# The first expert's operand from selection products on TensorE instead of a gather through HBM

## The chip, the cores and the metric

One core of one Trainium2 chip runs the whole program. The metric is the device time of one execution in microseconds (us). The kernel before took 1873.63 us in the median of 3 runs (1872.92 to 1876.07). Its profiled execution took 1871.54 us, with a span of 1869.7 us from the first to the last recorded instruction.

## The reference

Two blocks of a network work on 256 tokens of width 1024. What matters here is the last layer, a mixture of experts: a router picks 2 of 8 experts for each token, and each expert is a gated feed-forward network of inner width 3584.

```python
def moe_swiglu(h, w_router, w_gate, w_up, w_down):
    logits = (h @ w_router).astype(jnp.float32)
    top_vals, top_idx = lax.top_k(logits, TOP_K)
    top_w = jax.nn.softmax(top_vals, axis=-1)
    combine = jnp.einsum('bsk,bske->bse', top_w,
                         jax.nn.one_hot(top_idx, N_EXPERTS, dtype=jnp.float32)).astype(h.dtype)
    out = jnp.zeros_like(h)
    for e in range(N_EXPERTS):
        out = out + combine[..., e:e + 1] * swiglu(h, w_gate[e], w_up[e], w_down[e])
    return out
```

`h` is the root-mean-square norm of the layer's input with the gain `od_norm_ffn`, and `swiglu(h) = (silu(h @ w_gate) * (h @ w_up)) @ w_down`. All is float32.

## The kernel before

**Order of the work.** Each engine has its own list of instructions, written out in the program, and the engines wait for each other on semaphores. There is no scheduler: what stands first in a list goes first. The dense layers come first; the expert stage begins at about half of the span and lasts to nearly its end.

**Weights.** All weights stream through SBUF in granules of 128 x 2048 float32 (1 MB). SyncE loads them into six slots (`wraw`, L547 in the expert stage). ScalarE makes a rounded copy `whi` (L1320), VectorE the remainder `wlo` (L1382, the helper `lo`); both have three slots. TensorE forms each product in three matmuls, high by high, low by high and high by low (`three`, L656 to L658). A `wraw` slot is loaded again after `lo_done`; a `whi` slot is written again after TensorE has used it.

**Experts.** Each expert works on up to 128 tokens. One expert is 42 granules (`BODY`), in the order of the table `MOE`: gate and up projections of one of seven column groups, and the down projection of the group before. Gate and up take the tokens as the stationary operand `xgh`, `xgl` (model width on the partitions, tokens along the columns). An overflow path, which is not taken in the profiled execution, repeats the loop for experts with more than 128 tokens.

**Routing.** After the last job of the attention output, TensorE makes the logits (L895) and turns the residual to token-major form (L902). VectorE ranks the logits (`selm`, L1868, marks the chosen pairs). TensorE counts with a triangular matrix of ones how many tokens stand ahead of each token (L914 to L918, `slot_mm`). VectorE turns the counts into row numbers `row` of a table in HBM (`first_row` is 128 (e + 1), so expert 0 owns the rows 128 to 255) and into the indices `idx` (L1885). It then scales the tokens by norm and gain into `htm` (L1892 and L1893, two tiles of 128 tokens, `h_rows`).

**Dispatch.** GpSimd writes the tokens of `htm` to their rows of `expert_rows` in HBM with four indirect DMAs (L636, semaphore `dispatched`, 16 for each). ScalarE waits for all four and loads the 128 rows of expert 0 into `xgt` (L1288, L1289). TensorE waits for that load and transposes it in eight pieces (`turn_inputs(0)`, L926), four into bank 7 and four into bank 1. ScalarE makes `xgh` (L1294, `inputs_hi`), VectorE `xgl` (`inputs_lo`). Then the loop over the experts begins. The rows of expert E + 1 are loaded by SyncE during expert E, at its twentieth turn (L543 to L545), and transposed near its end (L981).

Of the kernel before, what the change touches and what calls it, by code (L numbers as in the profile page):

```python
# [15 lines left out]
P = 128  # L16
T = 256
D = 1024
# [9 lines left out]
NE = 8  # L28
# [263 lines left out]
def program(nc, wall, x_d, params_d, consts_d, pos_d, onehot_d, relb_d, poolw_d, recip_d, bv_d, fgain_d,  # L292
# [6 lines left out]
    with ctx:  # L299
# [11 lines left out]
        def sem(name):  # L311
            return ctx.enter_context(nc.semaphore(name))
# [27 lines left out]
        KB = 1024  # L340
# [70 lines left out]
        atl = place("atl", [P, 2, 4, P], f32r, 12 * KB)  # L411
        htm = place("htm", [P, 2, D], f32, 16 * KB)
        xtm = place("xtm", [P, 2, D], f32, 24 * KB)
        mgain = place("mgain", [P, D], f32, 32 * KB)
        fgain = place("fgain", [P, D], f32, 36 * KB)
        sg = place("sg", [P, 2, 512], f32, 40 * KB)
        act_ = place("act_", [P, 512], f32, 44 * KB)
# [11 lines left out]
        wrow = place("wrow", [P, 4], f32, 46 * KB + 704)  # L429
        cnt = place("cnt", [P, NE], f32, 46 * KB + 768)  # L430
        tabled = place("tabled", [P, 1], f32, 46 * KB + 832)
        cmp1 = place("cmp1", [P, 2, NE, NE], f32, 47 * KB)
        cmp2 = place("cmp2", [P, 2, NE, NE], f32, 47 * KB + 512)
        xgt = place("xgt", [P, D], f32, 48 * KB)
# [8 lines left out]
        ident = con[:, CC["ident"]:CC["ident"] + P]  # L443
        before = con[:, CC["before"]:CC["before"] + P]
        first_row = con[:, CC["first_row"]:CC["first_row"] + 2 * NE]

        def pcol(name, i):
            return par[:, COL[name] + i:COL[name] + i + 1]
# [37 lines left out]
        tok_var, tok_std, h_rows = sem("tok_var"), sem("tok_std"), sem("h_rows")  # L486
        logit_mm, routed_max, routed_exp = sem("logit_mm"), sem("routed_max"), sem("routed_exp")
        rank_done, slot_mm, flag_ready, idx_ready = sem("rank_done"), sem("slot_mm"), sem("flag_ready"), sem("idx_ready")
        zeros_set, rows_zeroed, dispatched = sem("zeros_set"), sem("rows_zeroed"), sem("dispatched")
        xg_loaded, xgt_mm, xg_hi, xg_lo = sem("xg_loaded"), sem("xgt_mm"), sem("xg_hi"), sem("xg_lo")  # L490
        gu_done, parts_used = sem("gu_done"), sem("parts_used")
# [32 lines left out]
        @block.sync  # L524
        def _(sp):
            sp.dma_start(wraw[:, 0, :], wall[0, :, :]).then_inc(w_loaded[0], 16)
            sp.dma_start(xres[:], x_d).then_inc(x_loaded, 16)
            sp.dma_start(par[:], params_d).then_inc(par_loaded, 16)
            sp.dma_start(wraw[:, 1, :], wall[1, :, :]).then_inc(w_loaded[1], 16)
            sp.dma_start(con[:], consts_d).then_inc(con_loaded, 16)  # L530
            sp.dma_start(posi[:], pos_d).then_inc(con_loaded, 16)
            for g in range(2, GD + 2):
                if g >= NW:
                    sp.wait_ge(lo_done, g - NW + 1)
                sp.dma_start(wraw[:, g % NW, :], wall[g, :, :]).then_inc(w_loaded[g % NW], 16)

            def load_expert(E, back):
                for j in range(2, BODY + 2):
                    g = GD + j
                    if j == 12:  # L540
                        sp.wait_ge(y_out, E * 2 + 2)
                        sp.dma_start(rows_out[bass.ds(E * P, P), :], ysb[:]).then_inc(y_stored, 16)
                    if j == 20:  # L543
                        sp.wait_ge(xgt_mm, E * 2 + 2)
                        sp.dma_start(xgt[:], rows_in[bass.ds(E * P + 2 * P, P), :]).then_inc(xg_loaded, 16)  # L545
                    sp.wait_ge(lo_done, E * BODY + (g - NW + 1))
                    sp.dma_start(wraw[:, g % NW, :],  # L547
                                 wall[bass.ds(E * BODY + (g - back * BODY), 1), :, :].rearrange("g p n -> (g p) n")
                                 ).then_inc(w_loaded[g % NW], 16)

            with sp.Fori(0, NE) as E:
                load_expert(E, 0)
            sp.wait_ge(flag_ready, 1)
            over = sp.value_load(flag[0:1, 0:1])
            with sp.If(over > 0):
                with sp.Fori(NE, 2 * NE) as E:
                    load_expert(E, NE)
                sp.wait_ge(y_out, 4 * NE + 2)
                sp.dma_start(rows_out[2 * NE * P:(2 * NE + 1) * P, :], ysb[:]).then_inc(y_last, 16)
            with sp.Else():  # L560
                sp.wait_ge(y_out, 2 * NE + 2)
                sp.dma_start(rows_out[NE * P:(NE + 1) * P, :], ysb[:]).then_inc(y_last, 16)
            for t in range(2):
                sp.wait_ge(fin_out, t + 1)
                sp.dma_start(out_d[t * P:(t + 1) * P, :], outb[:, t, :]).then_inc(stored, 16)
            sp.wait_ge(stored, 32)
# [84 lines left out]
        def _(pe):  # L651
# [258 lines left out]
            by_token(KD - 1)  # L910
            pe.wait_ge(rank_done, 1)

            count = bank[7][:, 32:32 + 3 * NE]
            nc.tensor.matmul(count[:, 0:8], before, selm[:, 0, :], start=True, stop=True)  # L914
            nc.tensor.matmul(count[:, 8:16], before, selm[:, 1, :], start=True, stop=False)
            nc.tensor.matmul(count[:, 8:16], ones[:], selm[:, 0, :], start=False, stop=True)
# [9 lines left out]
                        mm = nc.tensor.transpose(bank[b][:, c * P:(c + 1) * P], xgt[:, k * P:(k + 1) * P], ident)  # L926
                    mm.then_inc(xgt_mm, 1)

            turn_inputs(0)
            pe.wait_ge(xtm_out, 4)  # L930

            def expert(E):
                def part(j, out, c, half, last):

                    s = (GD + j) % NS
                    pe.wait_ge(lo_done, E * BODY + (GD + j + 1))
                    for i in range(4):
                        k = 4 * half + i
                        w = slice(i * 512, (i + 1) * 512)
                        mm = three(out, xgh[:, k, :], xgl[:, k, :], whi[:, s, w], wlo[:, s, w], k == 0, k == 7)  # L940
                    mm.then_inc(gu_done if last else parts_used, 1)

                def turn(c):

                    pe.wait_ge(prod_done, E * FC + (c + 1))
                    for i in range(4):
                        mm = nc.tensor.transpose(bank[6][:, i * P:(i + 1) * P], act_[:, i * P:(i + 1) * P], ident)  # L947
                    mm.then_inc(t_done, 1)

                def down(j, c, half):  # L950
                    s = (GD + j) % NS
                    pe.wait_ge(at_lo, E * FC + (c + 1))
                    if c == 0 and half == 0:
                        pe.wait_ge(y_out, E * 2 + 2)
                    pe.wait_ge(lo_done, E * BODY + (GD + j + 1))
                    for i in range(2):
                        k = 2 * half + i
                        for n in range(2):
                            w = slice(i * D + n * 512, i * D + (n + 1) * 512)
                            mm = three(bank[4 + n], ath[:, c % 2, k, :], atl[:, c % 2, k, :], whi[:, s, w], wlo[:, s, w],  # L960
                                       c == 0 and k == 0, c == FC - 1 and k == 3)
                    mm.then_inc(parts_used, 1)


                pe.wait_ge(xg_hi, E * 2 + 2)
                pe.wait_ge(xg_lo, E * 2 + 2)
                for j, (kind, c, half) in enumerate(MOE):
                    if kind == "G":
                        if half == 0 and c >= 2:
                            pe.wait_ge(silu_done, E * FC + (c - 1))  # L970
                        part(j, bank[c % 2], c, half, half == 1)
                    elif kind == "U":
                        if half == 0 and c >= 1:
                            turn(c - 1)
                        if half == 0 and c >= 2:
                            pe.wait_ge(prod_done, E * FC + (c - 1))
                        part(j, bank[2 + c % 2], c, half, half == 1)
                    else:
                        if c == FC - 1 and half == 0:
                            pe.wait_ge(at_lo, E * FC + FC)  # L980
                            turn_inputs(E + 1)  # L981
                        down(j, c, half)
                        if c == FC - 2 and half == 0:
                            turn(c + 1)
# [16 lines left out]
        def _(act):  # L1001
# [283 lines left out]
            for t in range(2):  # L1285
                sc.activation(ex[:, t, :], lg[:, t, :], ACT.Exp, bias=rs[:, t:t + 1], scale=rtm[:, t:t + 1]
                              ).then_inc(routed_exp, 1)
            act.wait_ge(dispatched, 64)  # L1288
            act.dma_start(xgt[:], rows_in[P:2 * P, :]).then_inc(xg_loaded, 16)  # L1289

            def inputs_hi(E):
                for half, b in ((0, 7), (1, 1)):
                    act.wait_ge(xgt_mm, E * 2 + (half + 1))
# [74 lines left out]
        def _(v):  # L1368
# [6 lines left out]
            def link(ins):  # L1375

                ins.then_inc(vstep, 1)
                chain[0] += 1
                v.wait_ge(vstep, chain[0])
# [494 lines left out]


            v.wait_ge(slot_mm, 1)
            counts = bank[7][:, 32:32 + 2 * NE].rearrange("p (t e) -> p t e", t=2)
            ve.tensor_scalar(spill[:], counts, P - 0.5, float(P * (NE - 1)), ALU.is_gt, MUL)
            link(ve.tensor_tensor(row[:], counts, first_row.rearrange("p (t e) -> p t e", t=2), ADD))
            link(ve.tensor_tensor(row[:], row[:], spill[:], ADD))  # L1880
# [3 lines left out]
            link(ve.tensor_tensor(rr[:, :, 0], rsum[:], rr[:, :, 1], SUB))  # L1884
            ve.tensor_copy(idx[:], rr[:].rearrange("p t r -> p (t r)")).then_inc(idx_ready, 1)  # L1885

            v.wait_ge(tok_std, 1)
            link(ve.reciprocal(rtm[:], rs[:, 12:14]))
            v.wait_ge(gains_loaded, 32)
# [3 lines left out]
                ve.scalar_tensor_tensor(htm[:, t, 512:1024], bank[b], rtm[:, t:t + 1], mgain[:, 512:1024], MUL, MUL  # L1893
                                        ).then_inc(h_rows, 1)

            link(ve.tensor_copy(cnt[:], bank[7][:, 32 + 2 * NE:32 + 3 * NE]))
            link(ve.tensor_reduce(rs[:, 2:4], lg[:], AX.X, MAX))
            link(ve.tensor_tensor(rs[:, 2:4], rs[:, 2:4], rtm[:], MUL))
            ve.tensor_scalar(rs[:, 0:2], rs[:, 2:4], -1.0, None, MUL).then_inc(routed_max, 1)
# [187 lines left out]
```

## Time and profile before

| what | us |
|---|---|
| median of 3 runs | 1873.63 |
| lowest, highest | 1872.92, 1876.07 |
| profiled execution | 1871.54 |
| its span | 1869.7 |
| TensorE busy in the span | 1725.9 (92%) |
| VectorE busy | 1464.0 (78%) |
| ScalarE busy | 1167.8 (62%) |
| GpSimd busy | 122.8 (7%) |

The table shows how full the engines are over the whole span. A change at one place is judged by the chain that ended last around that place: the profile's chain of waits names for each step the work that released it. The granted clock of TensorE (PEclk) is 1.00 at 2.4 GHz and 0.50 at 1.2 GHz. Starts are in microseconds from the start of the span.

### The profile page before, as it was taken

How to read it: one execution, taken by the hardware profiler on the slowest of the kernel's cores; microseconds unless marked ns; L12 is line 12 of the kernel's file. 1: busy time of each engine (PE TensorE's matmuls, PEld its weight loads, DVE VectorE, ACT ScalarE, POOL GpSimd, SP SyncE). 2: the span in 40 equal slices, each digit the busy share in tenths (PEclk: the TensorE clock that was granted, in tenths of full speed). 3: DMA queues.
4: the chain of work that ended last, by engine and by line, in shares of the span. 5: the costliest groups of instructions: out<-in, count | busy, mean ns of one | idle time of the engine just before them, and what ended most of it. 6: DMA issues, size and time to landing. Idle time of an engine off the chain costs nothing.

```text
span 1869.7 us, 26590 instructions
## 1 busy us (share of the span) xinstructions
PE 1725.9 (92%) x10284; PEld 1529.7 (82%) x10284; DVE 1464.0 (78%) x1444; ACT 1167.8 (62%) x1154; POOL 122.8 (7%) x112
## 2 busy tenths in 40 slices
PE   7787899997799999874999999999999999999994
PEld 6777799997799999764888888888888888888883
DVE  7888788866766655653888888889888888888886
ACT  5424567754254444443778778787787877877774
POOL 1000054421020001001000000000000000000000
PEclk9988999998999999897999999999999999999997
DMA  7332378584445457223899999999999999999994
GB/s 295 146 112 91 128 290 356 186 194 192 155 158 181 181 201 247 93 69 124 322 382 349 406 378 368 383 358 408 375 366 380 365 393 373 357 409 363 386 370 173
DMA packets 75741, 517.08 MB, mean 277 GB/s; under 512 B 8016, under 2 KB 8400, under 8 KB 17168
## 3 DMA queue, kind: packets, MB, share of 16 engines
q1 hardware_dynamic: 68976, 489.75, 68.8%
q0 software_dynamic: 6544, 25.74, 4.6%
q8 instruction: 53, 0.87, 0.2%
q10 hardware_dynamic: 144, 0.52, 0.1%
q14 instruction: 24, 0.20, 0.0%
HBM read 491.87 MB, written 24.12 MB: 276 GB/s over the span
## 4 chain that ended last, share of the span: by engine, by line
PE 80%; DVE 11%; ACT 5%; issue 2%; DMA 1%; POOL 1%; DVEq 0%; POOLq 0%; SPq 0%; ACTq 0%
PE psum L656 25%; PE psum L658 25%; PE psum L657 25%; DVE wlo L1382 4%; ACT whi L1012 3%; DVE acc L1497 2%; PE psum L947 1%; DVE al L1423 1%; PE psum L926 0%; ACT s L1229 0%; PE psum L706 0%; DMA expert_rows<-htm,idx 0%; DMA par<-params 0%; PE psum L863 0%; DMA yrow<-expert_outs,idx 0%
## 5 line engine op out<-in xcount | busy, mean ns | idle before, releaser
L1382 DVE TENSOR_TENSOR wlo<-wraw,whi 128x2048 fp32r<-128x2048 f32 x456 | 1043.2, 2291 | 242.4 <-ACT whi L1012 122.7
L1320 ACT ACTIVATE whi<-wraw 128x2048 fp32r<-128x2048 f32 x336 | 643.5, 1918 | 213.5 <-PE psum L658 213.5
L656 PE MATMUL psum<-ah,whi 128*128 128x256 f32 x1176 | 342.6, 291 | 20.8 <-DVE al L1423 11.9
L656 PE MATMUL psum<-whi,xgh 128*128 128x512 f32 x896 | 357.6, 399 | 1.6 <-DVE xgl L1382 1.6
L658 PE MATMUL psum<-whi,xgl 128*128 128x512 f32 x896 | 351.9, 393 | 0.0
L657 PE MATMUL psum<-wlo,xgh 128*128 128x512 f32 x896 | 349.8, 390 | 0.0
L657 PE MATMUL psum<-al,whi 128*128 128x256 f32 x1176 | 336.0, 286 | 0.0
L658 PE MATMUL psum<-ah,wlo 128*128 128x256 f32 x1176 | 335.7, 285 | 0.0
L1012 ACT ACTIVATE whi<-wraw 128x2048 fp32r<-128x2048 f32 x118 | 225.2, 1910 | 149.3 <-PE psum L658 145.6
L656 PEld LDWEIGHTS psum<-ah,whi 128*128 128x128 f32 x1176 | 229.5, 195 | 24.8 <-issue 10.4
L657 PEld LDWEIGHTS psum<-al,whi 128*128 128x128 f32 x1176 | 229.4, 195 | 0.6
L658 PEld LDWEIGHTS psum<-ah,wlo 128*128 128x128 f32 x1176 | 229.0, 195 | 0.0
L658 PEld LDWEIGHTS psum<-whi,xgl 128*128 128x128 f32 x896 | 168.6, 188 | 38.5
L656 PEld LDWEIGHTS psum<-whi,xgh 128*128 128x128 f32 x896 | 168.9, 188 | 36.9 <-issue 2.0
L657 PEld LDWEIGHTS psum<-wlo,xgh 128*128 128x128 f32 x896 | 168.9, 188 | 35.3
L656 PE MATMUL psum<-whi,ath 128*128 128x512 f32 x448 | 177.4, 396 | 0.0
L658 PE MATMUL psum<-whi,atl 128*128 128x512 f32 x448 | 175.6, 392 | 0.0
L657 PE MATMUL psum<-wlo,ath 128*128 128x512 f32 x448 | 174.5, 389 | 0.0
L658 PEld LDWEIGHTS psum<-whi,atl 128*128 128x128 f32 x448 | 84.1, 188 | 19.2
L657 PEld LDWEIGHTS psum<-wlo,ath 128*128 128x128 f32 x448 | 84.2, 188 | 18.1
L656 PEld LDWEIGHTS psum<-whi,ath 128*128 128x128 f32 x448 | 84.2, 188 | 16.9
L656 PE MATMUL psum<-fh,whi 128*128 128x256 f32 x352 | 97.5, 277 | 0.0
(330 smaller groups left out, 2070.0 us busy)
## 6 DMA issues: line engine op xcount, KB each, us to landing
wraw<-weights SPq DMA_DIRECT2D x456, 1024.0 KB, 6.8
expert_rows<-zeros POOLq DMA_DIRECT2D x1, 8704.0 KB, 43.5
expert_outs<-ysb SPq DMA_DIRECT2D x9, 512.0 KB, 6.6
expert_outs<-zeros POOLq DMA_DIRECT2D x1, 4096.0 KB, 59.8
xgt<-expert_rows SPq DMA_DIRECT2D x8, 512.0 KB, 8.2
bias_rows<-ttab POOLq DMA_DIRECT2D x1, 3072.0 KB, 36.5
btab<-bias_rows POOLq DMA_DIRECT2D x1, 2048.0 KB, 12.1
xres<-x SPq DMA_DIRECT2D x1, 1024.0 KB, 6.9
```

Source lines behind the costliest of these rows:

```text
L656: nc.tensor.matmul(out, lh, rh, start=start, stop=False)
L657: nc.tensor.matmul(out, lh, rl, start=False, stop=False)
L658: return nc.tensor.matmul(out, ll, rh, start=False, stop=stop)
L947: mm = nc.tensor.transpose(bank[6][:, i * P:(i + 1) * P], act_[:, i * P:(i + 1) * P], ident)
L1012: sc.activation(whi[:, g % NS, :], wraw[:, g % NW, :], ACT.Copy).then_inc(hi_done, 1)
L1320: sc.activation(whi[:, g % NS, :], wraw[:, g % NW, :], ACT.Copy).then_inc(hi_done, 1)
L1382: return ve.tensor_tensor(dst, value, hi.bitcast(f32), SUB)
L1423: ve.scalar_tensor_tensor(al[:, c, :], xres[:, c, :], gain(c), ah[:, c, :].bitcast(f32), MUL, SUB).then_inc(h_lo, 1)
L1497: ve.scalar_tensor_tensor(acc[:, c, :], u[:, c, tap:tap + T], pcol("conv_dw_w", 4 * tap + c), acc[:, c, :], MUL, ADD).then_inc(conv_step, 1)
```

## The change

The operand of expert 0 is no longer read back from HBM. VectorE compares the row numbers of expert 0 with the numbers 128 to 255 and gets two 0/1 matrices `sel0` (tokens on the partitions, places along the columns). TensorE multiplies `htm` with them: for each of the eight 128-wide pieces of the model width, two float32 matmuls of 128 x 128 (one for each tile of tokens) add up in PSUM, which gives the pieces in transposed form in the same banks as before. The numbers 128 to 255 come with the gain, whose tile `mgain` grows by 128 columns and moves. The counts move from bank 7 to bank 3. The four indirect writes stay, and SyncE now waits for them ahead of the load of the rows of expert 1.

```diff
@@ sync, load_expert
                     if j == 20:
+                        sp.wait_ge(dispatched, 64)
                         sp.wait_ge(xgt_mm, E * 2 + 2)
                         sp.dma_start(xgt[:], rows_in[bass.ds(E * P + 2 * P, P), :]).then_inc(xg_loaded, 16)
@@ tensor
-            count = bank[7][:, 32:32 + 3 * NE]
+            count = bank[3][:, 32:32 + 3 * NE]
...
-            turn_inputs(0)
+            pe.wait_ge(sel_ready, 1)
+            pe.wait_ge(h_rows, 2)
+            for half, b in ((0, 7), (1, 1)):
+                for c in range(4):
+                    k = 4 * half + c
+                    for t in range(2):
+                        mm = nc.tensor.matmul(bank[b][:, c * P:(c + 1) * P], htm[:, t, k * P:(k + 1) * P], sel0[:, t, :],
+                                              start=(t == 0), stop=(t == 1))
+                mm.then_inc(xgt_mm, 1)
             pe.wait_ge(xtm_out, 4)
...
-                            turn_inputs(E + 1)
+                            turn_inputs(E)
@@ scalar
-            act.wait_ge(dispatched, 64)
-            act.dma_start(xgt[:], rows_in[P:2 * P, :]).then_inc(xg_loaded, 16)
-
@@ vector
             ve.tensor_copy(idx[:], rr[:].rearrange("p t r -> p (t r)")).then_inc(idx_ready, 1)
 
+            v.wait_ge(gains_loaded, 32)
+            ve.tensor_scalar(sel0[:, 0, :], rows0, row[:, 0, 0:1], None, ALU.is_equal)
+            ve.tensor_scalar(sel0[:, 1, :], rows0, row[:, 1, 0:1], None, ALU.is_equal).then_inc(sel_ready, 1)
             v.wait_ge(tok_std, 1)
```

On TensorE, between the counts (`selm`) and the first matmul of expert 0 (`whi`, `xgh`), the list before reads:

```order
L918 MATMUL psum<-selm,ones 128x8
L926 MATMUL psum<-con,xgt 128x128 [waits xg_loaded]
L926 MATMUL psum<-con,xgt 128x128 x7
L986 UNCONDITIONAL_BRANCH [waits xtm_out]
L986 ISA
L936 ISA [waits xg_lo,xg_hi]
L656 MATMUL psum<-whi,xgh 128x512 [waits lo_done]
```

And now (`sel_150` is `sel0`):

```order
L923 MATMUL psum<-selm,ones 128x8
L940 MATMUL psum<-sel_150,htm 128x128 [waits h_rows,sel_ready]
L940 MATMUL psum<-sel_150,htm 128x128 x15
L999 UNCONDITIONAL_BRANCH [waits xtm_out]
L999 ISA
L949 ISA [waits xg_lo,xg_hi]
L661 MATMUL psum<-whi,xgh 128x512 [waits lo_done]
```

Eight transposes that waited for a load give way to sixteen matmuls that wait for VectorE. On VectorE, from the indices to the tokens, the list before reads:

```order
L1884 TENSOR_TENSOR rr<-rsum,rr 128x2 [waits vstep]
L1885 CAST idx<-rr 128x4 [waits vstep]
L1888 RECIPROCAL rtm<-rs 128x2 [waits tok_std]
L1892 SCALAR_TENSOR_TENSOR htm<-xtm,rtm,mgain 128x512 [waits xtm_out,gains_loaded,vstep]
L1893 SCALAR_TENSOR_TENSOR htm<-psum,rtm,mgain 128x512
```

And now:

```order
L1894 TENSOR_TENSOR rr<-rsum,rr 128x2 [waits vstep]
L1895 CAST idx<-rr 128x4 [waits vstep]
L1898 TENSOR_SCALAR sel_150<-mgain,row 128x128 [waits gains_loaded]
L1899 TENSOR_SCALAR sel_150<-mgain,row 128x128
L1901 RECIPROCAL rtm<-rs 128x2 [waits tok_std]
L1905 SCALAR_TENSOR_TENSOR htm<-xtm,rtm,mgain 128x512 [waits xtm_out,gains_loaded,vstep]
L1906 SCALAR_TENSOR_TENSOR htm<-psum,rtm,mgain 128x512
```

The two comparisons stand ahead of everything that makes `htm`; the rest of VectorE's list is as before.

## Rows read from the trace of the kernel before

**Rows 1.** Stretches: length, busy PE, PEld, DVE, ACT, POOL, clock, DMA share, GB/s.

```profile
799.80:802.00 2.20, 1.55 (x8) 1.12 (x8) 2.13 (x3) 0.00 (x0) 0.00 (x0) 1.00 0.00 0
...
859.20:860.80 1.60, 0.00 (x0) 0.00 (x0) 1.45 (x6) 1.58 (x5) 0.00 (x0) 0.91 1.00 425
...
864.00:884.00 20.00, 0.00 (x0) 0.00 (x0) 8.03 (x26) 3.15 (x5) 5.77 (x4) 0.50 0.53 184
...
887.60:891.20 3.60, 3.60 (x9) 2.83 (x10) 1.22 (x1) 3.31 (x5) 0.00 (x0) 0.50 0.00 0
...
900.00:1840.00 940.00, 940.00 (x4252) 771.40 (x4251) 826.61 (x457) 718.93 (x492) 0.00 (x0) 1.00 0.97 375
```

**Rows 2.** Chain of waits, 865 to 892: start, us, what.

```profile
865.39 0.67 DVE htm L1893
...
872.66 7.81 DMA expert_rows<-htm,idx
880.50 3.49 DMA xgt<-expert_rows
884.03 1.98 PE psum L926 x8
886.03 0.60 ACT xgh L1294
886.66 0.70 DVE xgl L1382
887.37 0.23 issue
887.60 0.79 PE psum L656
```

**Rows 3.** Timeline, VectorE: start, us, engine, line, what.

```profile
860.61 0.17 DVE L1868 TENSOR_SCALAR selm<-rank 128x16 f32<-128x16 f32 x1
...
866.63 0.75 DVE L1893 SCALAR_TENSOR_TENSOR htm<-psum,rtm,mgain 128x512 f32<-128x512 f32 x1
...
872.48 0.17 DVE L1914 TENSOR_REDUCE wrow<-ex 128x2 f32<-128x16 f32 x1
...
889.98 2.29 DVE L1382 TENSOR_TENSOR wlo<-wraw,whi 128x2048 fp32r<-128x2048 f32 x1 [2.62 <-ACT whi L1320]
```

**Rows 4.** VectorE's groups by form.

```profile
L1816 DVE TENSOR_SCALAR s<-s,st 128x128 f32<-128x128 f32 x16 | 4.5, 284 | 0.3
```

**Rows 5.** The load of the gains: duration ns, start us.

```profile
L628 POOL DMA_DIRECT2D mgain<-expert_gain x1: 561/561/561, 835.4 to 835.4; - x1
```

**Rows 6.** Timeline, TensorE.

```profile
784.39 0.90 PE L863 MATMUL psum<-con,s 128*128 128x128 f32 x3 [1.09 <-DVE s L1816]
...
786.36 0.63 PE L875 MATMUL psum<-p2T,v 128*128 128x128 f32 x2
786.79 0.63 PE L874 MATMUL psum<-p2T,v 128*128 128x128 f32 x2
...
788.72 0.34 PE L658 MATMUL psum<-ah,wlo 128*128 128x256 f32 x1
...
799.85 0.46 PE L855 MATMUL psum<-k,q 128*128 128x128 f32 x2 [2.08 <-issue]
...
830.99 0.39 PE L875 MATMUL psum<-p2T,v 128*128 128x128 f32 x2
831.21 0.39 PE L874 MATMUL psum<-p2T,v 128*128 128x128 f32 x2
...
860.84 0.60 PE L914 MATMUL psum<-selm,con 128*128 128x8 f32 x2 [1.71 <-DVE selm L1868]
...
891.44 0.39 PE L656 MATMUL psum<-whi,xgh 128*128 128x512 f32 x1
```

**Rows 7.** Waits from 887 to 1850: who, released by, us in total, times, longest.

```profile
ACT whi L1320 <- PE psum L658: 213.5, 297, 1.4
```

**Rows 8.** SyncE's timeline.

```profile
925.28 0.33 SPq L545 DMA_DIRECT2D xgt<-expert_rows  x1
```

More of the change, by code:

```diff
@@ L413, in program @@
         xtm = place("xtm", [P, 2, D], f32, 24 * KB)
-        mgain = place("mgain", [P, D], f32, 32 * KB)
+        mgain = place("mgain", [P, D + P], f32, 64 * KB)
         fgain = place("fgain", [P, D], f32, 36 * KB)
@@ L431, in program @@
         tabled = place("tabled", [P, 1], f32, 46 * KB + 832)
+        sel0 = place("sel0", [P, 2, P], f32, 32 * KB)
         cmp1 = place("cmp1", [P, 2, NE, NE], f32, 47 * KB)
@@ L445, in program @@
         first_row = con[:, CC["first_row"]:CC["first_row"] + 2 * NE]
+        rows0 = mgain[:, D:D + P]
         def pcol(name, i):
@@ L488, in program @@
         rank_done, slot_mm, flag_ready, idx_ready = sem("rank_done"), sem("slot_mm"), sem("flag_ready"), sem("idx_ready")
+        sel_ready = sem("sel_ready")
         zeros_set, rows_zeroed, dispatched = sem("zeros_set"), sem("rows_zeroed"), sem("dispatched")
@@ L1876, in _ @@
             v.wait_ge(slot_mm, 1)
-            counts = bank[7][:, 32:32 + 2 * NE].rearrange("p (t e) -> p t e", t=2)
+            counts = bank[3][:, 32:32 + 2 * NE].rearrange("p (t e) -> p t e", t=2)
             ve.tensor_scalar(spill[:], counts, P - 0.5, float(P * (NE - 1)), ALU.is_gt, MUL)
@@ L1894, in _ @@
                                         ).then_inc(h_rows, 1)
-            link(ve.tensor_copy(cnt[:], bank[7][:, 32 + 2 * NE:32 + 3 * NE]))
+            link(ve.tensor_copy(cnt[:], bank[3][:, 32 + 2 * NE:32 + 3 * NE]))
             link(ve.tensor_reduce(rs[:, 2:4], lg[:], AX.X, MAX))
@@ L2075 @@
         "final_gain": np.ascontiguousarray(np.broadcast_to(a["final_norm_2"][None, :], (P, D))),
-        "expert_gain": np.ascontiguousarray(np.broadcast_to(a["od_norm_ffn_2"], (P, D))),
+        "expert_gain": np.ascontiguousarray(np.broadcast_to(np.concatenate([a["od_norm_ffn_2"][0], np.arange(P, 2 * P, dtype=np.float32)]),
+                                                            (P, D + P))),
     }
```

## The prediction

> **What bounds the kernel now.** I read three views in order. First the stretches around the place of the change [rows 1]: TensorE has no instruction at all from 864 to 884 us, and from 900 to 1840 us, nearly the whole expert stage, it is busy without a break (940.00 of 940 us; 4252 records, 0.22 us each) at a granted clock of 1.00, which is 2.4 GHz. So the expert stage is bound by TensorE, and what shifts its first matmul shifts the end by as much, unless the stage then runs slower. Second the chain of waits across the gap [rows 2]: the second tile of `htm` is done at 867.4 us, four indirect writes follow, the last of them lands at 880.5 us, the read back takes 3.49 us, the eight transposes 1.98, then 0.60 + 0.70 + 0.23 us for the two halves of the operand, and the first matmul of expert 0 starts at 887.60 us. That is 20.2 us in which TensorE works for 2. Third the waits in the expert stage [rows 7]: ScalarE waits 213.5 us for TensorE to release slots, and no wait of ScalarE for a weight load is in that view, so loads are ahead.
>
> **The change, part by part.** The time of the profiled execution is 1871.54 us, 1.84 us more than its span. Its time lies 2.1 us under the median of the runs, 1873.63.
>
> *Two comparisons on VectorE, 128 x 128.* They stand ahead of `htm`. The nearest row is a TENSOR_SCALAR of the same shape that multiplies by a per-partition operand, 284 ns [rows 4]. Two instructions that don't wait for each other overlap a little: a `htm` of 0.75 us takes 0.67 us in the chain [rows 2, 3]. So I take 0.45 us for both (bounds 0.3 to 0.6). `htm` ends at 866.63 + 0.75 = 867.38 [rows 3], so now at 867.83. The wait for the gains is on loads of which the gain's was issued at 835.4 [rows 5], 29 us earlier, and holds nothing.
>
> *Sixteen float32 matmuls.* TensorE follows its releaser by 0.06 us (860.61 + 0.17 to 860.84) [rows 3, 6], so it starts at 867.9. One float32 matmul of 128 columns is two records. At 1.2 GHz the pair takes 786.79 - 786.36 = 0.43 us, at 2.4 GHz 831.21 - 830.99 = 0.22 us [rows 6]. The bounds are 16 x 0.22 = 3.5 and 16 x 0.43 = 6.9 us. The granted clock was 0.50 from 864 us on [rows 1], so they start slow. How soon the clock rises: in the attention stage TensorE took up float32 work at 784.39 at half clock, and the matmul at 788.72 is the first at short intervals again, 4.3 us later [rows 6]. I take 10 slow and 6 fast: 4.3 + 1.3 = 5.6 us, so the last ends at 873.5.
>
> *The two halves of the operand.* From the last transpose's end (886.01) to the first matmul it took 1.59 us [rows 2], and the same instructions follow now: first matmul of expert 0 at 875.1. VectorE must be free: its chain of small instructions ends at 872.65 [rows 3], now 873.1, and the two `xgl` after it need 0.70 + 0.75, then 0.23 of issue, so no speed of TensorE gives a start before 874.8. At 875.1 this wait just doesn't decide. **Gain so far 887.60 - 875.1 = 12.5 us.**
>
> *The clock at the start of the expert.* Before, nine matmuls ran at 0.50, from 887.60 to 891.44 = 3.84 us [rows 1, 2, 6]; at 0.23 us, a little over the stage's mean, they are 2.07. If the sixteen matmuls have raised the clock and it outlasts the pause of 1.6 us, this gives 1.75 us more. For that speaks the restart at 799.85: after an idle time of 2.08 us the clock was still 1.00 in the whole stretch to 802. Against it speaks the idle stretch from 859.2 to 860.8, in which it began to fall, 0.91 on the mean [rows 1, 6]. I take it as kept: **1.75 us.**
> The Trainium skill (TensorE: Matmul & The Clock Gate, Part 4, PE-mode transpose) says that transposes don't count as work for the clock as matmuls do. The trace agrees as far as it goes: the eight transposes at 884.03 were followed by the slow matmuls. By that rule the sixteen real matmuls are the better starter, which favours this term; without it the sum is 12.5.
>
> *What is late next.* The third granule's `wlo` ended at 889.98 + 2.29 = 892.27, 4.67 us after the first matmul [rows 3, 2], since ScalarE comes to it only behind the operand. Two granules are 24 matmuls: at full clock 24 x 0.23 = 5.5 us, so it is in time by 0.8 us; before, with 9 x 0.43 + 15 x 0.23 = 7.3, it was in time by 2.6. If this cover is gone each 0.1 us is paid once. Later granules follow TensorE's releases as before.
>
> *SyncE's new wait.* It stands ahead of the read for expert 1 at 925.28 [rows 8], now some 912, and behind it queue the remaining weight loads, for which ScalarE, VectorE and TensorE wait. The writes landed at 880.5, now 881: over 30 us of reserve, cost 0 beyond the handling of one instruction per expert, at most eight times 0.1 us and beside six slots of loads. ScalarE's read-back of 0.5 MB is gone and nobody needs it. The writes (to 881) lie beside the first granules, but no refill is issued before the third `wlo`, at 875.1 + 4.7 = 879.8, so there is about 1 us of overlap and 12 us until its granule is wanted. The counts in bank 3 and the 128 columns more in `mgain` change no wait: 0.
>
> **Sum:** 12.5 + 1.75 = 14.25 us. Profiled execution 1871.54 - 14.25 = 1857.3; span 1855.5; median 1873.63 - 14.25 = **1859.4**.
>
> **The rivals.**
> *A, the forecast:* 1859.4, with its own range 1857 to 1861.5 (the clock may rise 1 to 2 us earlier or later; the floor of 874.8 allows 14.55, a rise near the end of the sixteen leaves 13.2).
> *B, the clock isn't there at the expert's start:* it falls in the pause (12.5 gained) or never rises in the sixteen (start 867.9 + 6.9 + 1.6 = 876.4, 11.2 gained). 1861 to 1862.4. The fall around 860 us speaks for it [rows 1].
> *C, loads pace the expert stage.* The DMA engines show a share of 0.97 at 375 GB/s in the stage [rows 1]. Then the end hangs on when the first refill is issued; that is 4.7 us behind the first matmul before and after, so the 12.5 stay, and the 1.75 are lost: 1861.1. Against it, ScalarE's waits are all on TensorE [rows 7].
> The Trainium skill (DMA: Bandwidth & Descriptors, Where 436 GB/s comes from) puts the HBM limit of a core at about 358 GB/s, which would make loads the bound; the trace shows 375 over 940 us, and the measurement decides.
> *D, the change doesn't do what it says:* the first matmul is held by another condition, as VectorE's routing chain. In the trace this ends at 872.65 [rows 3], 15 us before the present start, so something unseen would have to hold it: 1873.6.
> *E, slower:* one mechanism, the price of the sixteen matmuls. Weights of float32 that change with every matmul and a moving operand just written might cost far more than the rows of the attention stage show. With the 1.75 also lost, the break-even is (887.60 - 1.59 - 867.9) / 16 = 1.13 us for each, and at 1.36 us it is slower by 0.2%; at four times the slow row, 1.72 us, the start would be at 897.0, 9.4 us late: 1883. The rows of 0.43 us, with changing weights as well, speak against it.
>
> **How the numbers follow.** A 0.66, B 0.20, C 0.05, D 0.05, E 0.04. A change within 0.2% (3.7 us) can't be told from none. A, B and C are all faster by more: 0.91; D is the same, 0.05; E slower, 0.04. Before's runs lie between 1871.5 and 1876.1, so a median may sit 2 us off by itself: low 1857.0 and high 1864.5 leave out D, E and the tails of the rest.
>
> **What would show it.** Right: no instruction of TensorE from 863.2 to 867.9, then the sixteen (32 records) over 5 to 6.5 us, with pairs at 0.43 and then 0.22; first expert matmul at 875 to 875.5 at a granted clock of 1.00; 0.22 per matmul from there on, and the end 14 us earlier with the stage's length 1.75 us shorter. Wrong: pairs above 1 us; a matmul of expert 0 that waits for `wlo` of the third granule; a wait of ScalarE for a weight load; SyncE held at the twentieth turn of expert 0.

## The result, and the profile after

The changed kernel takes 1858.89 us in the median of 4 runs (1857.89 to 1860.72), against 1873.28 us before (4 runs, 1871.30 to 1876.07). The ratio is 0.9922 with a 95% interval of 0.991 to 0.9933, so it is faster by 14.4 us. Forecast were 1859.4 us and 14.25 us less. The profiled execution took 1860.72 us, where 1857.3 was forecast.

The chain of waits of the profile after, across the same place (start, us, what), answers to [rows 2]:

```profile
869.72 0.67 DVE htm L1906
870.53 5.28 PE psum L940 x32
875.83 0.61 ACT xgh L1304
876.46 0.70 DVE xgl L1392
877.16 0.23 issue
877.39 0.49 PE psum L661
```

The writes and the read back are gone from the chain. TensorE stands still for 4.8 us instead of 20.9, and the sixteen products take 5.28 us. The timeline of VectorE and TensorE (start, us, engine, line, what) answers to [rows 3] and [rows 6]:

```profile
863.23 0.17 DVE L1878 TENSOR_SCALAR selm<-rank 128x16 f32<-128x16 f32 x1
...
867.06 0.28 DVE L1898 TENSOR_SCALAR sel<-mgain,row 128x128 f32<-128x128 f32 x1
867.26 0.28 DVE L1899 TENSOR_SCALAR sel<-mgain,row 128x128 f32<-128x128 f32 x1
867.46 0.16 DVE L1901 RECIPROCAL rtm<-rs 128x2 f32<-128x2 f32 x1
...
875.48 0.17 DVE L1927 TENSOR_REDUCE wrow<-ex 128x2 f32<-128x16 f32 x1
875.69 1.47 DVE L1392 TENSOR_TENSOR xgl<-psum,xgh 128x512 fp32r<-128x512 f32 x2
...
879.78 2.29 DVE L1392 TENSOR_TENSOR wlo<-wraw,whi 128x2048 fp32r<-128x2048 f32 x1 [2.63 <-ACT whi L1330]
```

The two comparisons push what follows by 0.40 us. VectorE is busy with the routing chain to 875.65 and goes into the first `xgl` at once; the `xgh` that it needs was ready at 874.64, so the first `xgl` was held by VectorE's own list. The stretches (length, busy PE, PEld, DVE, ACT, POOL, clock, DMA share, GB/s) answer to [rows 1]:

```profile
870.50:872.00 1.50, 1.47 (x7) 1.50 (x8) 1.43 (x4) 1.48 (x2) 1.20 (x2) 0.50 0.31 126
872.00:873.00 1.00, 1.00 (x6) 1.00 (x6) 1.00 (x1) 0.99 (x3) 1.00 (x1) 0.50 0.82 336
873.00:874.00 1.00, 1.00 (x8) 1.00 (x8) 0.83 (x6) 0.01 (x1) 1.00 (x1) 0.71 0.00 0
874.00:875.00 1.00, 1.00 (x12) 1.00 (x11) 0.86 (x5) 0.60 (x1) 0.70 (x2) 1.00 1.27 156
875.80:877.40 1.60, 0.01 (x1) 0.01 (x1) 1.27 (x2) 1.55 (x2) 0.82 (x1) 1.00 0.88 323
...
877.40:1833.93 956.53, 956.50 (x4320) 784.49 (x4320) 839.03 (x464) 733.13 (x504) 0.00 (x0) 1.00 0.96 373
```

The clock rose inside the products, stayed up over the pause of 1.6 us, and the whole expert stage ran at 1.00. The same stretch of the kernel before, from its first expert matmul to its end, had as many matmuls and took 1.54 us more:

```profile
887.60:1845.67 958.07, 958.03 (x4320) 785.75 (x4320) 839.02 (x464) 733.14 (x504) 0.00 (x0) 1.00 0.96 370
```

**How the two profiled executions add up.** Their spans differ by 10.9 us only (1869.7 to 1858.8), though the runs differ by 14.4. I measure from the start of `selm`, the ranks, which lies ahead of all that was changed. In the profile after it came 2.62 us later (863.23 against 860.61); up to there both programs do the same work. From the ranks to expert 0: 26.99 before, 14.16 after, 12.83 less. Expert stage (its first matmul to the end of its last): 1.53 less. From there to the end of the span: 24.03 and 24.87, 0.84 more. So -12.83 - 1.53 + 0.84 + 2.62 = -10.9. Over the fourteen profiles of this study the ranks start between 860.07 and 864.30 us. A single pair of spans is therefore uncertain by as much as a small term, and from here on each profile is read by the two distances, in us. "Count pairs" are the five pairs of counting matmuls behind the ranks; they are slow where the clock fell ahead of them.

| profile | ranks to expert 0 | expert stage | count pairs | clock at expert 0 |
|---|---|---|---|---|
| before | 26.99 | 958.07 | slow | slow |
| after | 14.16 | 956.54 | slow | full |
| after, second profile (e8) | 13.06 | 956.67 | fast | full |
| after, third profile (e11) | 13.08 | 956.36 | fast | full |
| e1 | 25.26 | 957.91 | fast | full for five matmuls, then slow |
| e2 | 17.20 | 957.99 | slow | slow |
| e3 | 16.71 | 956.30 | fast | full |
| e4 | 13.19 | 964.68 | fast | full |
| e5 | 14.21 | 956.41 | slow | full |
| e6 | 12.96 | 957.76 | fast | slow |
| e7 | 11.68 | 956.33 | fast | full |
| e9 | 13.19 | 956.47 | fast | full |
| e10 | 11.69 | 956.33 | fast | full |
| e12 (e7 again) | 11.68 | 956.45 | fast | full |

The unedited changed kernel stands in two groups, 14.16 and 13.07, by the clock of the five pairs of counting matmuls: 0.43 or 0.22 us for each. Before and after both have slow pairs, so their 12.83 us compare like with like.

Why the ranks themselves come earlier or later was not tested. A lower clock in the stages ahead is likely a part of it. In `after` and in e8, the same program, one `wlo` of the attention stage starts 0.30 us apart (760.42 and 760.12), the next 3.12 us apart (802.09 and 798.97). In between the clock differed (after, then e8; the columns of [rows 1]):

```profile
760.00:780.00 20.00, 14.02 (x82) 12.25 (x81) 12.98 (x34) 8.97 (x30) 0.00 (x0) 0.74 0.23 92
...
760.00:780.00 20.00, 13.26 (x91) 12.07 (x90) 13.20 (x34) 10.01 (x35) 0.00 (x0) 0.91 0.23 86
```

### The profile page after: what moved, and what is told of

Its sections match the earlier page's. It is cut to its first block, busy times and chain, and to the rows that moved or that the text cites. A ratio compares the mean times of both kernels' runs of the same rounds, so it can differ in the third digit from the quotient of the medians.

```text
span 1858.8 us, 26648 instructions
## 1 busy us (share of the span) xinstructions
PE 1732.1 (93%) x10308; PEld 1535.2 (83%) x10308; DVE 1464.2 (79%) x1446; ACT 1167.8 (63%) x1154; POOL 122.7 (7%) x112
## 4 chain that ended last, share of the span: by engine, by line
PE 80%; DVE 12%; ACT 5%; issue 2%; DMA 1%; POOL 0%; DVEq 0%; POOLq 0%; SPq 0%; ACTq 0%
PE psum L661 25%; PE psum L663 25%; PE psum L662 25%; DVE wlo L1392 4%; ACT whi L1025 3%; DVE acc L1507 2%; PE psum L960 1%; DVE al L1433 1%; PE psum L711 1%; ACT s L1242 0%; DMA par<-params 0%; PE psum L931 0%; DMA yrow<-expert_outs,idx 0%; PE psum L868 0%; POOL ssum L582 0%
## 5 line engine op out<-in xcount | busy, mean ns | idle before, releaser
L661 PEld LDWEIGHTS psum<-ah,whi 128*128 128x128 f32 x1176 | 230.9, 196 | 26.7 <-issue 10.4
## 6 DMA issues: line engine op xcount, KB each, us to landing
btab<-bias_rows POOLq DMA_DIRECT2D x1, 2048.0 KB, 12.8
```

The costliest lines, as they stand in the source:

```text
L661: nc.tensor.matmul(out, lh, rh, start=start, stop=False)
```

## Experiments

My theory was that of the prediction. The rivals tested were that the clock is no term of its own (e1), that the read and not the wait for the writes made the round trip long (e2), that a product costs far more than 0.43 us or is hidden (e3), and that loads pace the expert stage (e4, e9). From e5 on the question was what bounds the start of expert 0 now. A ratio is to the kernel before on the same chip, where the changed kernel has 0.9922.

**e1, filler in the kernel before.**

```diff
+            for _ in range(76):
+                nc.tensor.matmul(bank[0], oh2[:, 0, 0:P], oh2[:, 0:2, :].rearrange("p a b -> p (a b)"), start=True, stop=True)
             turn_inputs(0)
```

> The kernel before with 76 matmuls more (128 x 512, results unused) on TensorE between the counts and the eight transposes, where it only waits. They end at about 863.2 + 9 x 0.43 + 67 x 0.23 = 882.5 us, before the load lands at 884.0. Theory (the clock at the expert's start is a term of its own): transposes in about 1.0 us instead of 1.98 and the first nine matmuls of expert 0 at the short interval, 2.07 instead of 3.84 us: 2.7 us faster than before, about 1870.6. Rival (the shorter stage after the change has another cause): the clock doesn't help, 1873.3, or the filler delays the transposes and it is slower.

Measured: 1873.08 us (11 runs) against 1873.99, ratio 0.9994 (0.9985 to 1.0003). The gain of 2.7 us did not come; the median is 0.9 us lower, and the interval includes none. TensorE's timeline shows why:

```profile
886.16 1.09 PE L926 MATMUL psum<-con,xgt 128*128 128x128 f32 x8 [1.79 <-DMA xgt<-expert_rows]
889.09 0.50 PE L656 MATMUL psum<-whi,xgh 128*128 128x512 f32 x1 [1.83 <-DVE xgl L1384]
889.42 0.39 PE L657 MATMUL psum<-wlo,xgh 128*128 128x512 f32 x1
...
890.76 0.63 PE L656 MATMUL psum<-whi,xgh 128*128 128x512 f32 x1
...
893.75 0.40 PE L657 MATMUL psum<-wlo,xgh 128*128 128x512 f32 x1
```

The transposes took 1.09 instead of 1.98 us, as expected. The expert began at full clock but fell to the slow interval after five matmuls and stayed there for eight. Ahead of the fall stand two idle times of 1.8 us with only the transposes between them; that they cost the clock, a little late, is the likely reading, and no run takes them apart. So a full clock at the first matmul doesn't yet mean that it stays, and this run doesn't price the clock: that it is worth 1.5 us must come from the stage lengths of the table, 956.3 to 956.7 where it was kept and 957.8 to 958.1 where it was not, leaving out e4.

The Trainium skill (TensorE: Matmul & The Clock Gate, Part 4, PE-mode transpose) says that transposes don't count as work for the clock in the way that matmuls do. This run agrees with that, but would look the same if they counted and were too few.

**e2, the read without the wait for the writes.**

```diff
-            act.wait_ge(dispatched, 64)
-            act.dma_start(xgt[:], rows_in[P:2 * P, :]).then_inc(xg_loaded, 16)
+            act.dma_start(xgt[:], wall[0, :, 0:D]).then_inc(xg_loaded, 16)
@@ sync, j == 20
+                        sp.wait_ge(dispatched, 64)
```

> The kernel before, but ScalarE's load of the first operand reads 128 rows of the weights in HBM instead of the rows just written, and so needs no wait for the four indirect writes (SyncE waits for them ahead of the rows of expert 1). Expert 0 works on other numbers. It keeps one HBM read and the transposes. Theory (most of the gain is the wait for the writes): the load is issued at 870.0, lands at about 873.6, transposes to 875.6, first matmul of expert 0 at 877.2: 10.4 us earlier, clock still slow at the start: about 1863. So this would be some 4 us behind the changed kernel. Rival (the round trip through HBM costs by the read, slowed by the writes beside it): the load lands at 878 or later and the gain is under 6 us, 1867 or more.

Measured: 1864.87 us, ratio 0.9951 (0.9938 to 0.9964). That is 9.1 us faster than before, where 10.4 were expected; the rival's 6 or less is excluded, though it holds a part of the truth. The chain of waits:

```profile
870.69 6.08 DMA xgt<-weights
```

The load took 6.08 us beside the writes and a weight load, not 3.49 as behind them [rows 2]. It reads other rows of HBM, of the same number and size. Of the 12.8 us that the change takes out between ranks and expert 0, 9.8 (26.99 - 17.20) go with the wait for the writes, net of the 2.6 us by which the read got slower; the other 3.0 go with the read and the transposes, less what the products cost.

**e3, the products twice.**

```diff
+                for again in range(2):
```

(around the loop over `c`)

> The changed kernel with the sixteen selection matmuls done twice into the same places (32, same result). Theory (they stand on the path, and cost by the clock): the profiled sixteen took 5.28 us with the clock rising on the way; the second sixteen all run at 0.22 us: first matmul of expert 0 later by 3.5 us, about 1862.4. Rival E of the prediction (a float32 product with new weights costs over 1 us each): later by 16 us, 1875. Rival (hidden behind VectorE's routing chain): 1858.9.

Measured: 1861.75 us, ratio 0.994 (0.9928 to 0.9952), 2.9 us above the changed kernel's 1858.89 where 3.5 were expected. The 64 records took 8.81 us, 3.5 more than the 32, and the distance from the ranks is 3.65 above that of the profiles with fast counts. The second sixteen are on the path at 0.22 us each at full clock, so they are neither hidden nor dear: rival E is refuted.

**e4, SyncE's wait early.**

```diff
+                    if j == 2:
+                        sp.wait_ge(dispatched, 64)
...
                     if j == 20:
-                        sp.wait_ge(dispatched, 64)
```

> The changed kernel with SyncE's wait for the four indirect writes moved from the twentieth turn to the first weight load of the expert loop, so that no refill is issued until the writes have landed. Theory (the wait has a long reserve): the writes land at about 884 us and only one load is held, by some 10 us; its granule is wanted some 12 us after that: 0, 1858.9. Rival (loads pace the expert stage): what the refills lose is not made up, 2 to 10 us slower, 1861 to 1869.

Measured: 1866.3 us, ratio 0.9964 (0.9951 to 0.9977), 7.4 us slower than the changed kernel's 1858.89. The expectation was wrong, and by the edit: the loop's first six loads (j from 2 to 7) are issued ahead of the first expert matmul, so not one load was held but six. SyncE issued none of them before 877.40, when the writes had landed. The waits after the start of the stage show what came of it (who, released by, us, times, longest):

```profile
ACT whi L1331 <- DMA wraw<-weights: 7.0, 2, 6.6
```

The stage grew to 964.68 us, 8.1 more. TensorE waited 5.71 us at the third granule, and the clock was lost in this wait:

```profile
886.61 0.79 PE L662 MATMUL psum<-whi,xgh 128*128 128x512 f32 x1 [5.71 <-DVE wlo L1393]
...
891.88 0.39 PE L662 MATMUL psum<-whi,xgh 128*128 128x512 f32 x1
```

The twelve matmuls from 886.61 to 891.88 took 5.27 us, 2.5 more than at 0.23 us each. So 5.7 of the 8.1 us are the wait, and the rest is the clock behind it. Nothing of the delay was caught up later. The writes themselves landed in 3.7 us in the median, against 7.8 beside a weight load in the profile after.

**e9, the same wait where e4 was meant to have it.** `j == 8` instead of `j == 2`.

> The changed kernel with SyncE's wait for the writes at the seventh weight load of the expert loop, the first that is issued after the first matmul of expert 0 (behind the six that e4 held back unmeant). Theory (the reserve of the wait is long where it stands, and it was the six held loads that cost e4 8 us): the writes land about 3 us after the moment at which this load would be issued at most, its granule is wanted 12 us later: no wait of ScalarE for a load, stage 956.5 us, 1858.9. Rival (any held load is paid, since loads pace the stage): stage longer by 1 to 3 us.

Measured: 1859.30 us against 1858.45 for the changed kernel on the same chip; ratios 0.9931 (0.9917 to 0.9945) and 0.9925 (0.9911 to 0.9938), no difference. The stage is 956.47 us. The view of ScalarE's waits, the counterpart of [rows 7], has no load in it:

```profile
ACT whi L1331 <- PE psum L664: 212.1, 296, 0.9
```

How long was the load held? SyncE's timeline, the changed kernel and then e9:

```profile
882.24 0.33 SPq L552 DMA_DIRECT2D wraw<-weights  x1
...
883.28 1.78 SPq L553 DMA_DIRECT2D wraw<-weights  x2
```

In the changed kernel it follows the end of the third `wlo` by 0.17 us (882.07), in e9 by 1.50 (881.78), so the wait held it for 1.3 us. That is less than the 3 us that were expected at most, and a stage paced by loads would be 1.3 us longer; it is not. So this delay costs nothing at the first refill, and the wait at the twentieth turn holds nothing. The expert stage is not paced by loads once its first six granules are there. The Trainium skill (DMA: Bandwidth & Descriptors, Where 436 GB/s comes from) gives about 358 GB/s as the HBM limit of a core. The stage of the changed kernel moved 373 GB/s over 956.5 us, more than that, and the measurement decides.

**e5, the routing chain late.** The instructions from `v.wait_ge(routed_exp, 2)` to the last `wrow` are moved behind `inputs_lo(0)`.

> The changed kernel with VectorE's chain that makes the routing weights (from the wait for routed_exp on, ten small instructions) moved behind the two halves of xgl. Theory (after the change TensorE's end and VectorE's chain are level: the second xgh ends at 876.43, VectorE's first xgl at 876.4): the second xgl still waits for ScalarE, 0, 1858.9. Rival (VectorE's chain bounds the start): the first xgl moves up to 874.7 and the start by more than 0.5 us.

Measured: 1857.80 us, ratio 0.9918 (0.9905 to 0.9932): not told apart from the changed kernel. The distance is 14.21 with slow counts, 0.05 from the 14.16 of after. As expected, the second `xgl` waits for ScalarE (1.10 us in this profile).

**e6, fillers ahead of the counts (6) and of the products (18), in the form of e1's.**

> The changed kernel with 6 unused matmuls (128 x 512) ahead of the counts and 18 between the counts and the selection products, to keep TensorE's clock up. Theory: the five count pairs at 0.22 instead of 0.43 give 1.05 us; the sixteen products take 3.5 instead of 5.28 us, but VectorE's chain then bounds: first xgl from 874.6, start of expert 0 at 876.3 instead of 877.4: 1.1 us faster than the changed kernel, 1857.8. Rival (no floor at VectorE): 2.8 us, 1856.1. Rival (fillers cost as much as they give): 1858.9 or more.

Measured: 1859.99 us, ratio 0.9924 (0.991 to 0.9938), no gain where 1.1 us was expected. The 32 records took 3.81 us instead of 5.28, but VectorE entered the first `xgl` only at 875.73, behind its routing chain, and so the pause grew:

```profile
870.57 3.81 PE L944 MATMUL psum<-sel,htm 128*128 128x128 f32 x32 [0.56 <-DVE htm L1910]
877.26 0.79 PE L661 MATMUL psum<-whi,xgh 128*128 128x512 f32 x1 [2.88 <-DVE xgl L1396]
```

The start moved by 1.2 us against the profile after and by 0.1 against those with fast counts. In the pause of 2.88 us the clock fell, and the stage took 957.76. What was won ahead of the stage was given back in it.

**e7, both edits**, and **e12**, the same again beside the changed kernel (**e11**).

> Both edits of the two runs before this: the routing chain behind xgl, and the fillers. Theory (the two bounds stand side by side, so only both together move the start): counts 1.05 us earlier, sixteen products in 3.5 us, start of expert 0 at 877.4 - 1.05 - 1.75 = 874.6: 2.8 us faster than the changed kernel, 1856.1. Rival (edits are independent): the sum of what each gave alone.

> e7 once more beside the changed kernel on one chip, since e7 and e10 disagree (1855.2 and 1857.8, with the same start of expert 0 in their profiles). Theory (fillers and late routing chain give 1.4 to 2.5 us at the start of expert 0): 1.5 to 2.5 us faster than the changed kernel beside it, about 1856.5, in every part of the spread. Rival (e7's 1855.2 was a draw of the rest of the program): no difference, 1858.5.

> The changed kernel a third time, as the partner of the run beside it on one chip: 1858.5.

The distance is 11.68 in both profiles, the stage 956.33 and 956.45. Against profiles with fast counts the start is 1.4 us earlier, against the slow one 2.5. So both edits together move what neither moved alone: the theory of two level bounds holds. Of the 2.8 us expected of e7, reckoned from the slow profile, 2.5 came in its profile. Timed, e7 took 1855.20 us, ratio 0.9897 (0.9883 to 0.9912), e12 1857.38, ratio 0.9916 (0.9902 to 0.993), and e11 beside it 1858.47, ratio 0.992 (0.9907 to 0.9934). The direct comparison of e12 with e11 gives 1.1 us, less than the 1.5 to 2.5 expected and within the spread.

**e10, e7 with five matmuls more in the pause**, and **e8**, the changed kernel beside it.

> e7 (routing chain late, fillers ahead of the counts and the products) with 5 unused matmuls more in the pause between the products and the first matmul of expert 0. Theory (the clock at the expert's start is kept or lost by chance over the pause, 1.7 us): start 11.7 us after the ranks as in e7, stage 956.4 in every execution: profile like e7, median 0 to 1 us below it, about 1855. Rival (the fillers delay the start): start later than 11.7.

> The changed kernel once more, for a comparison on the same chip with the two runs beside it: 1858.9 as first measured, ratio to before 0.992. Start of expert 0 14.2 us after the ranks (selm), stage 956.5 us if the clock is kept over the pause, 958 if not.

e10 took 1857.79 us, ratio 0.9924 (0.991 to 0.9938), where about 1855 was expected; e8 took 1858.45, ratio 0.9925. The distance of e8 is 13.06 and not the 14.2 expected, since its counts were fast. The distance of e10 (11.69) and its stage (956.33) are e7's. The filler does no harm, and its use could not be seen, since e7 kept the clock in both its profiles as well. That e7 or e10 beats the changed kernel is likely from the profiles and not shown by the runs: the medians of e7, e12 and e10 lie 0.7 to 3.7 us below 1858.5 to 1858.9, the executions of e7 and e12 spread from 1852.19 to 1859.36.

## Why the prediction was right

**The gap.** Taken from the ranks, the start moved by 12.83 us where 12.5 were summed. The comparisons cost 0.40 (0.45 said). The products took 5.28 (5.6 said): the clock rose within 873 to 874, some 3 us after their start, not 4.3. From their end to the first matmul it took 1.58 (1.59 said).

**The clock.** 1.53 us of 1.75. The first two matmul intervals after are 0.34 and 0.22 us, before 0.59 and 0.43. The term rested on an even choice between two rows, and it fell right: a pause of 1.6 us kept the clock in all nine profiles with the products and that pause (after, e3, e4, e5, e7, e8, e9, e11, e12), and 2.88 us lost it in e6. Rival B is a real case at a longer pause.

**The floor at VectorE.** The prediction put the earliest start that VectorE allows 0.3 us ahead of the forecast start. In the profile after they are level, since the products ended earlier: the second `xgh` ends at 876.44, and VectorE's first `xgl` some 0.05 us before. e5, e6 and e7 show both bounds.

**The cover of the third granule.** Its `wlo` ended at 879.78 + 2.29 = 882.07, 4.68 us after the first matmul (4.67 said), and TensorE didn't wait.

**SyncE's wait and the loads.** No cost, shown by e9 for a hold of 1.3 us. The prediction's argument against rival C held. e4 shows where the reserve ends: six loads held until the writes have landed cost 8 us, 5.7 by the wait and the rest by the clock, all of it kept to the end.

**Sum.** 12.83 + 1.53 = 14.36 us by the two distances, 14.4 by the medians, 14.25 forecast. That the three agree within 0.2 us is partly luck: the counts alone are worth 1.1 us by the state of the clock, and the tail differed by 0.84. What was missing from the working is this scatter: the single profiled pair gave 10.9, and the profiled execution came 3.4 us above its forecast of 1857.3.

## What to carry to other kernels

A small operand that goes to HBM and back only to be permuted can be made by a 0/1 matrix product on the engine that waits for it; count the wait for the writes first, it was 9.8 of the 12.8 us here. Compare two profiles from an instruction just ahead of the edit, not from the start of the span, since the same instruction started up to 4.2 us apart between these profiles. Before filling or moving one engine's work, look whether a second engine ends within a few tenths of it: then only both edits together move the start, and one alone can lengthen a pause and lose the clock.

## What the runs showed of the hardware

Four indirect writes of 128 rows (2 MB together) landed in 7.8 us in the median beside a 1 MB load, in 3.7 us without one (e4). A 0.5 MB load took 3.49 us alone (before) and 6.08 beside the writes and a 1 MB load (e2).

In e1 the clock fell not in the pause but about 1.2 us after work had begun again, at 890.3 (0.83 on the mean from 890.2 to 890.4, 0.50 behind it): five matmuls ran at full clock, then eight at half. A look at the first matmul alone would have called it kept.
